# Constant products between the first transposes, and router products of two tiles ahead of the seventh projection

## The chip, the cores and the metric

The kernel runs on one core of one Trainium2 chip. A core has five engines that run side by side, each with its own instruction queue: TensorE (PE: matrix products and transposes), VectorE (DVE), ScalarE (ACT), GpSimd (POOL, here used to issue DMAs, among them the indirect ones) and SyncE (SP, which only issues DMAs). They signal each other with semaphores. The metric is the device time of one execution in microseconds; lower is better.

## The reference, cut to what matters

The program is one layer of a streaming encoder on 512 tokens of width 1024, with 16 learned meta tokens in front, all in float32:

```python
h   = rmsnorm(concat(meta, x), mix_norm)
u   = h @ w_in                      # 1024 -> 2304, split among three groups of heads
mix = concat(conv(u), windowed_attention(u), gated_recurrence(u))
r   = concat(meta, x) + mix @ w_out
n   = rmsnorm(r, ffn_norm)
group  = top1(softmax(n @ w_router_group + b));   expert = top2(softmax(n @ w_router_expert + b) in that group)
y   = sum of weight * (silu(n @ w_gate[e]) * (n @ w_up[e])) @ w_down[e] over the two experts
out = rmsnorm(r + y, final_norm)[16:]
```

There are 32 experts of 3 MB of weights each, and every one of them is loaded.

## The kernel before

**Mixer.** The 512 tokens are four tiles of 128 rows. In the beginning each tile of x is normalised (ScalarE: squares, Ln, Exp; DVE: the scaling, `normed_x`, L723) and transposed by TensorE in eight 128x128 blocks (`turn_tile`, L1220 to L1224); small parameters (L1234) and the meta tokens (L1238) are transposed too. DVE and ScalarE copy the transposes out, and `half_product` (L1226) starts the input projection with the gate columns: eight products over the 1024 inputs, each shown in the trace as two passes of 264 columns. The other projections, the convolution, the recurrence and the attention follow; TensorE's order is written out by hand in `mixer_tensor`.

**Output projection and router.** `project(i)` (L1442) is the output projection of tile i//2, half i%2 of the columns: eight products of 512 columns into bank 7, 16 passes in the trace (L1455). `residual(i)` (L923 to L930, DVE) adds bank 7 to the residual tile, and the next `project` waits for it, since all use bank 7. `second_norm(j)` (L653, ScalarE) makes the factor of the second norm. `normed_rows(j)` (L932 to L938, DVE) multiplies the tile by it and by the gain into `xf`; POOL then writes this tile to the memory tensor `normed` (L1551 to L1553). `router_turn(j, n)` transposes the two halves of the residual tile, `router_half` copies them out, and `router_of(j)` (L1496) does the router's products: eight products of only 36 columns, 16 passes in the trace (L1471). The seventh and eighth projection are `project(6)` and `project(7)`, the two halves of the last tile.

**Experts known early.** `select` (L957, DVE) turns the router's outputs of tiles 0 to 2 into picks. TensorE counts them (`early_ranks`, L1501), DVE and TensorE build lists from them (`early_rows`, `early_lists`, `early_index`), and POOL gathers rows of `normed` by these lists with an indirect DMA (`rows_in`, L2000 to L2006). POOL waits for the three written tiles (L2019) and for the index (L2020) before the first gather. The last tile takes the same path a little later: TensorE transposes the first gathered block (L1536, seen in the trace as L1560) ahead of the last four router products (L1538).

**Experts.** Weights go through a ring of seven slots. SP issues the load of a slot once TensorE's last block on it is done (L1638 to L1641). The first six experts' weights are asked for during the mixer, each behind the wait that frees its place: `load_down(5)` and `load_gate(5)` behind projection 6 (L468 to L470), `load_down(0)` and `load_up(5)` behind projection 7 (L471 to L473).

Banks are PSUM, TensorE's output memory. The queues are in order: on each engine an instruction that waits holds back all behind it.

Of the kernel before, what the change touches and what calls it, by code (L numbers as in the profile page):

```python
# [13 lines left out]
P = 128  # L14
D = 1024
KT = D // P
# [147 lines left out]
def trunk(nc, x, meta_tokens, mix_norm, w_in, conv_dw_w, conv_dw_b, conv_ln_g, conv_ln_b, attn_sinks,  # L164
# [3 lines left out]
    with ctx:  # L168

        def sb(name, shape, dt=F32, of=ctx):  # L170
            return of.enter_context(nc.sbuf_tensor(name, shape, dt))
# [4 lines left out]
        bank = [ctx.enter_context(nc.psum_tensor(f"bank{i}", [P, 512], F32)) for i in range(8)]  # L176
# [4 lines left out]
        cst = sb("cst", [P, K_ALL])  # L181
# [75 lines left out]
        ident = cst[:, K_ID:K_ID + P]  # L257
# [148 lines left out]
        def turned(j, k):  # L406

            c = k % 2 * 2 * P + j % 2 * P
            return bank[(2, 3, 4, 5)[k // 2] if j < 2 else (6, 7, 4, 5)[k // 2]][:, c:c + P]
# [293 lines left out]
        def mixer_vector(dve):  # L703
            vn = [0]

            def step(ins):
                vn[0] += 1
                ins.then_inc(v_step, 1)
                dve.wait_ge(v_step, vn[0])

            def mark(ins):
                vn[0] += 1
                ins.then_inc(v_step, 1)
                return vn[0]
# [31 lines left out]
            for i in range(2):  # L746
                n = f"a{i}"
# [175 lines left out]
            def residual(i):  # L923

                j, n = i // 2, i % 2
                dve.wait_ge(oproj, i + 1)
                if i == 0:
                    dve.wait_ge(d_resid, 16)
                h = xs[:, j, n * 512:(n + 1) * 512]
                V.tensor_tensor(h, h, bank[7][:, :], ALU.add).then_inc(h2_done, 1)  # L930

            def normed_rows(j):  # L932
                if j == 0:
                    dve.wait_ge(d_gain, 16)
                dve.wait_ge(h2_done, 2 * j + 2)
                dve.wait_ge(fstat, j + 1)
                V.scalar_tensor_tensor(out=xf[:, j, :], in0=xs[:, j, :], scalar=rstd[:, j:j + 1], in1=gain,
                                       op0=ALU.mult, op1=ALU.mult).then_inc(xf_ready, 1)  # L938

            def router_half(j, n=0):  # L940
                dve.wait_ge(xfT, 2 * j + n + 1)
                src = bank[TURN_BANK[j, n]][:, :].rearrange("p (k t) -> p k t", k=4)
                dst = mixT[:, 4 * n:4 * n + 4, j * P:(j + 1) * P] if j < NT - 1 or n else h_low
                V.tensor_copy(dst, src).then_inc(hfT_v, 1)
# [75 lines left out]
            def early_rows():  # L1020

                dve.wait_ge(ranks, 1)
                step(V.tensor_tensor(early_of, picked[:, :, 0:ET, 0:SLOTS],
                                     rank_early[:, :, 0:SLOTS].unsqueeze(1).to_broadcast([P, 2, ET, SLOTS]), ALU.mult))
                step(V.tensor_reduce(early_row, early_of, AX, ALU.add))
                by_row = [P, 2 * ET, ROWS_A]
                V.tensor_tensor(early_slot, cst[:, K_IOTA:K_IOTA + ROWS_A].unsqueeze(1).to_broadcast(by_row),
                                early_row.rearrange("p k j -> p (k j)").unsqueeze(2).to_broadcast(by_row), ALU.is_equal).then_inc(match, 1)
# [44 lines left out]
            router_half(2)  # L1073
            for k in range(2):
                mark(V.tensor_scalar(tok2[:, k], cst[:, K_TOK:K_TOK + NT], float(k * SEQ - FAR), None, ALU.add))
            normed_rows(2)
            select(range(ET), bank[0], ET)
            dve.wait_ge(picks, ET)
            dve.wait_ge(v_step, vn[0])
# [4 lines left out]
            mark(V.memset(sum3_late[:, 0:SLOTS], 0.0))  # L1084
            mark(V.tensor_copy(sum3_late[:, SLOTS:], sum3[:, SLOTS:]))
            residual(6)
            early_rows()
            router_half(3)
            early_index()
# [126 lines left out]
        def mixer_tensor(pe):  # L1216
            T = nc.tensor
            pe.wait_ge(d_cst, 16)

            def turn_tile(j):  # L1220
                pe.wait_ge(xn_ready, NORMS.index(j) + 1)
                for k in range(KT):
                    ins = T.transpose(turned(j, k), xs[:, j, k * P:(k + 1) * P], ident)
                ins.then_inc(xT_done, 1)  # L1224

            def half_product(n, h):  # L1226
# [2 lines left out]
                                   start=(k == 0), stop=(k == KT - 1))  # L1229
                return ins  # L1230

            turn_tile(0)
            pe.wait_ge(d_par, 112)
            T.transpose(bank[6][:, 0:86], rows[:, :], ident[0:86, 0:86]).then_inc(par_T, 1)  # L1234
            turn_tile(1)
            pe.wait_ge(xn_ready, NORMS.index(NT) + 1)
            for k in range(KT):
                ins = T.transpose(bank[7][:, k * META:(k + 1) * META], meta_x[:, k * P:(k + 1) * P], ident[0:META, 0:META])  # L1238
            ins.then_inc(metaT, 1)
            pe.wait_ge(d_win[0], 16)  # L1240
            pe.wait_ge(hT_v, 5)
            pe.wait_ge(hT_a, 4)
# [199 lines left out]
            def project(i, ks=range(KT)):  # L1442

                j, n = i // 2, i % 2
                if i == 0:
                    pe.wait_ge(y_c, 2)
                    pe.wait_ge(y_h, 2)
                if n == 0:
                    pe.wait_ge(y_a, 2 * j + 2)
                if j == 0:  # L1450
                    pe.wait_ge(d_wout[n], 16)
                if i >= 1:
                    pe.wait_ge(h2_done, i)
                for k in ks:
                    ins = T.matmul(bank[7][:, :], mixT[:, k, j * P:(j + 1) * P], w_out_sb[:, n, k, :],  # L1455
                                   start=(k == 0), stop=(k == KT - 1))
                if k == KT - 1:
                    ins.then_inc(oproj, 1)

            def router_turn(j, n):  # L1460
                pe.wait_ge(h2_done, 2 * j + n + 1)
                for k in range(4):
                    ins = T.transpose(bank[TURN_BANK[j, n]][:, k * P:(k + 1) * P], xs[:, j, (4 * n + k) * P:(4 * n + k + 1) * P], ident)
                ins.then_inc(xfT, 1)
# [31 lines left out]
            def router_of(j):  # L1496
                pe.wait_ge(hfT_a, j + 1)
                pe.wait_ge(hfT_v, j + 1)
                router(j, bank[0], range(KT)).then_inc(logits, 1)

            def early_ranks():  # L1501

                pe.wait_ge(picks, ET)
                o = bank[1]
                T.matmul(o[:, 0:3 * NE], tri, both[:, 0:3, :], start=True, stop=False)
                T.matmul(o[:, NE:3 * NE], ones, both[:, 0:2, :], start=False, stop=False)
                T.matmul(o[:, 2 * NE:3 * NE], ones, both[:, 0, :], start=False, stop=True).then_inc(ranks, 1)
# [12 lines left out]
            router_of(0)  # L1520
            router_turn(2, 0)
            router_turn(2, 1)
            project(6, range(KT // 2))
            router_of(1)
            router_of(2)
            project(6, range(KT // 2, KT))
            early_ranks()
            router_turn(3, 0)
            project(7, range(3))
# [543 lines left out]
        @block.vector  # L2073
        def _(dve):
            experts_vector(dve, *mixer_vector(dve))

        @block.tensor
        def _(pe):
            mixer_tensor(pe)
            experts_tensor(pe)  # L2080
# [33 lines left out]
```

## Time and profile before

| | us |
|---|---|
| median of 3 runs (lowest, highest) | 558.34 (555.75, 558.54) |
| profiled execution, its own time | 555.7 |
| span of its trace | 553.8 |
| TensorE busy | 489.0 (88%) |
| DVE busy | 247.0 (45%) |
| ScalarE busy | 152.3 (28%) |
| mean granted TensorE clock | 0.957 |
| bytes moved by DMA | 142.69 MB, mean 258 GB/s |

The span runs from the first to the last instruction; the profiled execution's own time is 1.9 us longer. Shares of busy time are averages over stages that have different limits. The page cuts the span into 40 slices of 13.8 us each and gives a digit for each. The groups of rows further down are read from the page and from the trace.

### The profile page before, as it was taken

The page shows a single profiled execution, that of the slowest core. Times are in us where ns is not written, and L with a number is a line of the kernel's source. Part 1 is how long each engine was busy: PE and PEld are TensorE (multiplying, and loading weights), DVE is VectorE, ACT ScalarE, POOL GpSimd, SP SyncE. Part 2 cuts the span into 40 slices and gives each one's busy share as a digit, 9 for nine tenths or more (in the row PEclk, how much of TensorE's full clock was granted, in tenths as well). Part 3 has the DMA queues.
Part 4 walks back from the last instruction along what each step waited for, and adds up shares of the span by engine and source line. Part 5 has one row for each costly group of instructions (what it writes and reads, how often), then busy time and mean ns, then how long its engine had stood idle before and what let it go on. Part 6 is the DMA issues. An engine that isn't in the chain of part 4 may idle for free. (4 is left out here: it accounts for less than half of the span.)

```text
span 553.8 us, 11004 instructions
## 1 busy us (share of the span) xinstructions
PE 489.0 (88%) x4555; PEld 310.6 (56%) x4555; DVE 247.0 (45%) x608; ACT 152.3 (28%) x375; POOL 40.0 (7%) x47
## 2 busy tenths in 40 slices
PE   3999999999999999999999999999999697856800
PEld 3885478875557656557476655655555354443400
DVE  3206995767236854634573333323332123112237
ACT  5410004766012623422033322222221112011123
POOL 0010000000001000000110111211112011000000
PEclk9999999999999999998999999999999899789865
DMA  7990000000007797008888999999999999999465
GB/s 264 363 351 1 2 0 2 0 1 1 2 1 228 278 423 299 39 38 290 347 302 327 340 418 392 402 415 413 419 413 415 410 413 416 410 415 408 176 261 209
DMA packets 38754, 142.69 MB, mean 258 GB/s; under 512 B 5170, under 2 KB 12584, under 8 KB 30384
## 3 DMA queue, kind: packets, MB, share of 16 engines
q1 hardware_dynamic: 31824, 127.89, 59.0%
q0 software_dynamic: 5760, 11.55, 5.8%
q10 hardware_dynamic: 1120, 2.54, 1.2%
q8 instruction: 37, 0.61, 0.4%
q14 instruction: 13, 0.11, 0.1%
HBM read 135.83 MB, written 15.20 MB: 273 GB/s over the span
## 5 line engine op out<-in xcount | busy, mean ns | idle before, releaser
L1455 PE MATMUL bank<-area_w,area_m 128*128 128x512 f32 x128 | 58.5, 609 | 0.4 <-issue 0.4
L1567 PE MATMUL bank<-area_g,area_m 128*64 128x256 f32 x352 | 47.0, 413 | 7.9 <-DMA area_g<-in_w_exp_up 7.9
L1567 PE MATMUL bank<-area_w,area_m 128*64 128x256 f32 x256 | 34.0, 408 | 7.4 <-DMA area_w<-in_w_exp_up 7.1
L1567 PEld LDWEIGHTS bank<-area_g,area_m 128*64 128x64 f32 x352 | 25.7, 147 | 25.3 <-issue 14.2
L762 DVE SCALAR_TENSOR_TENSOR area_m<-area_g,cols,area_m 128x512 f32<-128x512 f32 x60 | 39.8, 745 | 0.0
L1455 PEld LDWEIGHTS bank<-area_w,area_m 128*128 128x128 f32 x128 | 24.1, 195 | 27.5 <-issue 27.5
L1770 DVE COPY cst<-bank 128x128 f32<-128x128 f32 (+1 forms) x39 | 10.2, 260 | 59.2 <-PE bank L1584 39.9
L1286 PE MATMUL bank<-area_h,area_w 128*128 128x264 f32 x160 | 35.9, 386 | 0.0
L1286 PEld LDWEIGHTS bank<-area_h,area_w 128*128 128x128 f32 x160 | 30.4, 190 | 5.6 <-issue 0.5
L1320 PE MATMUL bank<-area_h,area_w 128*128 128x512 f32 x64 | 30.8, 612 | 0.0
L1567 PEld LDWEIGHTS bank<-area_w,area_m 128*64 128x64 f32 x256 | 18.9, 145 | 18.7 <-issue 11.7
L1288 PE MATMUL bank<-area_h,area_w 128*128 128x512 f32 x64 | 27.6, 592 | 0.0
L1704 ACT ACTIVATE cst<-bank 128x128 f32<-128x128 f32 x22 | 6.2, 280 | 74.5 <-PE bank L1567 74.5
L1788 DVE COPY area_m<-bank 64x512 f32<-64x512 f32 x20 | 13.9, 694 | 24.3 <-PE bank L1590 22.5
L2011 POOL DMA_INDIRECT expert_out<-area_m,cst x14 | 13.8, 987 | 150.1 <-DVE area_m L1791 107.6
L1575 PE MATMUL bank<-area_w,area_m 128*32 128x128 f32 x640 | 21.6, 275 | 2.5 <-DMA area_w<-in_w_exp_up 2.5
L1777 DVE TENSOR_TENSOR cst<-cst,bank 128x128 f32<-128x128 f32 x22 | 6.4, 289 | 38.1 <-ACT cst L1704 38.1
L1575 PEld LDWEIGHTS bank<-area_w,area_m 128*32 128x32 f32 x640 | 16.5, 109 | 8.9 <-issue 7.0
L1674 ACT ACTIVATE area_m<-bank 128x512 f32<-128x512 f32 x17 | 10.2, 599 | 40.6 <-PE bank L1560 34.7
L1278 PE MATMUL bank<-area_w,area_h 128*128 128x128 f32 (+1 forms) x128 | 21.3, 327 | 0.0
L1590 PE MATMUL bank<-area_g,cst 128*64 128x512 f32 x88 | 21.1, 599 | 0.0
L1288 PEld LDWEIGHTS bank<-area_h,area_w 128*128 128x128 f32 x64 | 12.2, 190 | 14.9 <-issue 14.8
(356 smaller groups left out, 780.6 us busy)
## 6 DMA issues: line engine op xcount, KB each, us to landing
area_w<-in_w_exp_gate SPq DMA_DIRECT2D x14, 1024.0 KB, 14.6
area_w<-in_w_exp_up SPq DMA_DIRECT2D x14, 1024.0 KB, 21.3
area_g<-in_w_exp_gate SPq DMA_DIRECT2D x14, 1024.0 KB, 15.8
area_g<-in_w_exp_up SPq DMA_DIRECT2D x14, 1024.0 KB, 23.2
area_g<-in_w_exp_down SPq DMA_DIRECT2D x14, 1024.0 KB, 23.2
area_w<-in_w_exp_down SPq DMA_DIRECT2D x14, 1024.0 KB, 22.5
area_w<-in_w_in SPq DMA_DIRECT2D x7, 1024.0 KB, 12.6
area_w<-in_w_out SPq DMA_DIRECT2D x2, 2048.0 KB, 12.4
```

The costliest lines, as they stand in the source:

```text
L762: ins = V.scalar_tensor_tensor(out=mixT[:, i, :], in0=src, scalar=w, in1=mixT[:, i, :], op0=ALU.mult, op1=ALU.add)
L1278: ins = T.matmul(out_b[:, n0:n0 + w], hT[:, k, t0:t0 + P], w_in_sb[:, k, c0:c0 + w], start=(k == 0), stop=(k == KT - 1))
L1286: ins = T.matmul(half_of(n, h), w, hT[:, k, h * HALF:(h + 1) * HALF], start=(k == 0), stop=(k == KT - 1))
L1288: ins = T.matmul(out_b[:, :], w, hT[:, k, META:], start=(k == 0), stop=(k == KT - 1))
L1320: ins = T.matmul(bank[QUERY_BANK[i]][:, :], w_in_sb[:, k, C_Q + i * P:C_Q + (i + 1) * P], hT[:, k, META:], start=(k == 0), stop=(k == KT - 1))
L1455: ins = T.matmul(bank[7][:, :], mixT[:, k, j * P:(j + 1) * P], w_out_sb[:, n, k, :], start=(k == 0), stop=(k == KT - 1))
L1567: ins = T.matmul(out_b[h * BC:(h + 1) * BC, 0:2 * P], x[:, k, :], w_gate_up[slot][:, :, k, h * P:(h + 1) * P], start=(k == 0), stop=(k == ...
L1575: ins = T.matmul(out_b[q * 32:(q + 1) * 32, 0:P], x[:, k, :], w_gate_up[slot][:, q // 2, k, q % 2 * P:(q % 2 + 1) * P], start=(k == 0), st ...
L1590: ins = T.matmul(out_b[n * BC:(n + 1) * BC, :], aT[:, f * BC:(f + 1) * BC], w_down[slot][:, f, n * 512:(n + 1) * 512], start=(f == 0), sto ...
L1674: A_.activation(xT_half(i, 0), bank_half(0)[:, :, 0:rows_of(i)], ACT.Copy).then_inc(xT_lo, 1)
L1788: V.tensor_copy(y_part(yb[k.i % 2], k.row, 1), src[BC:P, :]).then_inc(y_hi, 1)
L2011: Q.indirect_dma_start(expert_out, index_of(i, idx_es, idx_s), yb[i % 2], None, bounds_check=2 * SEQ - 1, oob_is_err=False).then_inc(d_sc[ ...
```

## The change

Three edits. `fill(n)` issues n products of the identity with 256 columns of the constant table (identity and ones) into bank 1, which nothing reads before the first input projection overwrites it; four stand ahead of the first tile's transposes, one behind them, three ahead of the first projection. TensorE now does the router products of tiles 1 and 2 ahead of the whole of `project(6)`, where it did the first half of the projection before them and the second behind them. And DVE does `normed_rows(2)` behind `residual(6)`, no longer ahead of `select`.

```diff
@@ mixer_vector
-            normed_rows(2)
             select(range(ET), bank[0], ET)
             dve.wait_ge(picks, ET)
...
             residual(6)
+            normed_rows(2)
             early_rows()
@@ mixer_tensor
+            def fill(n):
+
+                for _ in range(n):
+                    T.matmul(bank[1][:, 0:2 * P], ident, cst[:, 0:2 * P], start=True, stop=True)
+
+            fill(4)
             turn_tile(0)
+            fill(1)
             pe.wait_ge(d_par, 112)
             T.transpose(bank[6][:, 0:86], rows[:, :], ident[0:86, 0:86]).then_inc(par_T, 1)
             turn_tile(1)
...
             ins.then_inc(metaT, 1)
+            fill(3)
             pe.wait_ge(d_win[0], 16)
...
             router_turn(2, 1)
-            project(6, range(KT // 2))
             router_of(1)
             router_of(2)
-            project(6, range(KT // 2, KT))
+            project(6)
             early_ranks()
```

## Rows read from the trace of the kernel before

**Rows 1.** The page, part 2: two lines of the 40 slices, in tenths.
```profile
PEclk9999999999999999998999999999999899789865
DMA  7990000000007797008888999999999999999465
```

**Rows 2.** Busy time by stage: stage, length, engines' busy time, clock, DMA share, GB/s.
```profile
306.00:308.00 2.00, 2.00 (x19) 1.12 (x19) 0.50 (x3) 1.50 (x4) 0.57 (x1) 1.00 0.57 80
...
350.00:500.00 150.00, 133.75 (x1594) 78.16 (x1585) 40.55 (x99) 29.70 (x72) 19.09 (x19) 0.94 1.02 413
```

**Rows 3.** Timeline, 4 to 32 us: start, duration, engine, line, operation, idle before.
```profile
4.11 1.28 ACT L498 ACT_TABLE_LOAD   x1 [4.11 <-DMA cst<-in_table]
...
8.04 1.94 PE L1223 MATMUL bank<-cst,area_x 128*128 128x128 f32 x8 [8.04 <-DVE area_x L723]
...
10.54 1.97 PE L1223 MATMUL bank<-cst,area_x 128*128 128x128 f32 x8 [0.41 <-DVE area_x L723]
...
12.43 1.03 PE L1238 MATMUL bank<-cst,area_g 16*128 16x16 f32 x8
...
14.54 5.04 PEld L1228 LDWEIGHTS bank<-area_h,area_w 128*128 128x128 f32 x16 [1.19 <-DMA area_w<-in_w_in]
14.58 5.43 PE L1228 MATMUL bank<-area_h,area_w 128*128 128x264 f32 x16 [1.11 <-DVE area_h L739]
...
21.59 10.85 PE L1228 MATMUL bank<-area_h,area_w 128*128 128x264 f32 x48
```

**Rows 4.** Timeline of TensorE, 250 to 280 us.
```profile
252.80 3.60 PE L1455 MATMUL bank<-area_w,area_m 128*128 128x512 f32 x8
256.24 3.66 PE L1471 MATMUL bank<-cst,area_m 128*128 128x36 f32 x32
259.73 5.38 PE L1455 MATMUL bank<-area_w,area_m 128*128 128x512 f32 x8
265.37 0.46 PE L1505 MATMUL bank<-cst 128*128 128x96 f32 x2 [0.27 <-DVE cst L1003]
...
267.26 0.66 PE L1463 MATMUL bank<-cst,area_x 128*128 128x128 f32 x4 [1.03 <-DVE area_x L930]
267.75 2.74 PE L1455 MATMUL bank<-area_w,area_m 128*128 128x512 f32 x6
...
277.34 1.15 PE L1560 MATMUL bank<-cst,area_h 128*128 128x128 f32 x8
```

**Rows 5.** Busy time by stage, with the granted clock, around the second half projection.
```profile
260.00:266.00 6.00, 5.73 (x14) 2.34 (x13) 5.90 (x49) 0.00 (x0) 0.00 (x0) 0.72 1.00 410
```

**Rows 6.** Timeline of DVE, 255 to 268 us.
```profile
255.30 1.29 DVE L937 SCALAR_TENSOR_TENSOR area_h<-area_x,stat,gain_out 128x1024 f32<-128x1024 f32 x1 [1.89 <-ACT stat L657]
...
259.94 0.58 DVE L962 SCALAR_TENSOR_TENSOR cst<-bank,stat,rbias 128x36 f32<-128x36 f32 x3 [3.35 <-PE bank L1471]
...
264.76 0.56 DVE L1003 SCALAR_TENSOR_TENSOR cst<-cst 128x32 f32<-128x32 f32 x3
...
266.52 0.68 DVE L930 TENSOR_TENSOR area_x<-area_x,bank 128x512 f32<-128x512 f32 x1
```

**Rows 7.** DMAs: issues by POOL, share of queue 0 (262 to 263 us), time to landing.
```profile
256.88 0.53 POOL L1553 DMA_DIRECT2D normed<-area_h  x1 [11.73 <-DVE area_h L937]
272.92 1.07 POOL L2005 DMA_INDIRECT area_h<-normed,cols  x1 [15.51 <-DVE cols L1033]
...
DMA to landing us min/median/max: 2.9/2.9/8.3
...
q0 software_dynamic: 37, 0.15, 36.8%
...
area_h<-normed,cols POOLq DMA_INDIRECT x1, 4.4
...
area_h<-normed,cols POOLq DMA_INDIRECT x1, 6.0
```
The line of minimum, median and maximum is that of the writes to `normed` at L1553; the last two lines are the gathers issued at 272.92 and 274.30.

## The prediction

> **What bounds the kernel now.** I read four views in turn. The slices of the page first [rows 1]: the reader is to see that the DMA engines idle in the middle of the mixer and are full for the last half, and that the granted TensorE clock dips once in slice 19, at about 260 us. Then busy time by stage [rows 2]: in 306 to 308 us the DMA share is 0.57, from 350 to 500 us it is 1.02 at 413 GB/s. The kernel therefore has two parts. From 308 us on the stream of expert weights sets the end, and nothing changes in it. Ahead of that, each load waits for TensorE to free a slot, so a microsecond won or lost by TensorE before about 306 us moves the start of the full stream, and with it the end, one for one. Then the timeline of TensorE: from 14.58 us it works with almost no gap up to 265 us, so the mixer is TensorE's too and a gain at its start is carried through. Last, the timeline and the DMAs between 250 and 280 us, where the rest of the change lies.
>
> **Part 1, the eight constant products.** TensorE waits for nothing but the first table part, which has landed by 4.11 us, and then stands until 8.04 us [rows 3]. A 264-column pass takes 10.85/48 = 0.226 us in the 48 from 21.59 us on; the 16 from 14.58 us take 5.43 us instead of 3.62 [rows 3]. They begin near 0.45 us each and end at 0.226, the ratio of the two clock levels, 1.2 and 2.4 GHz: TensorE starts at the lower and reaches the upper inside this group. A constant product is two passes of 256 columns.
> - fill(4): 8 passes at 0.44 = 3.5 us, 4.1 to 7.6, in front of DVE's first tile at 8.04. Cost 0.
> - fill(1): 0.44 us at the upper level, 0.9 at the lower, in a group that ends at about 9.8 and whose successor waits for DVE until 10.54 [rows 3]. Cost 0 to 0.3.
> - fill(3): 6 passes, 1.3 or 2.6 us, from about 13.2. The product behind it could start at 14.54, when the first weights land [rows 3]. Cost 0.1 at the upper level, 1.5 at the lower.
>
> If the clock is up by 8 us and stays up, the 16 passes take 3.62 us: 1.8 won, 0.1 paid, so **-1.7 us**. Bounds: +1.5 (the clock doesn't rise, fill(3) is pure delay) and -3.6 (an execution in which all 16 passes would have run low, 16 x 0.226). I take -1.7, the value of this profile.
>
> The Trainium skill (TensorE: Matmul & The Clock Gate, "What's actually happening") says the array's default is the lower clock and that sustained activity releases it; by it fill(4) alone should raise the clock before the first transposes. The trace shows only the rise inside the first dense group, not what a filler does.
>
> **Part 2, the order of router products and the seventh projection.** Before: half projection 252.80 to 256.24, 32 router passes to 259.7, half projection to 265.1, ranks at 265.37 after the picks [rows 4]. The first half needed 3.44 us (0.43 a pass), the second 5.38: the mean granted clock of 260 to 266 us is 0.72, which is 3.4 us at the lower level [rows 5], a loss of 1.9. After: router passes 252.8 to 256.5, then 16 passes of projection, 6.9 us, and the same 1.7 to 1.9 of low clock, since the weak stretch is now longer, not shorter. TensorE reaches the ranks at 265.0 to 265.2. So the projection gains nothing by itself (-1.8 if the low stretch should vanish, +1.5 if the router passes themselves run low too). DVE's select starts at 256.6 instead of 259.94 and its picks are made at 262.0 instead of 265.3 [rows 6]; TensorE's wait of 0.27 goes. The larger effect: the residual of the seventh projection no longer queues behind the select (266.52) but follows the projection at 265.2, so TensorE's next transposes start at 266.0 instead of 267.26 [rows 4]. From there the eighth projection, lists and index come 1.2 us earlier, and TensorE reaches the transposes of the first gathered block at 276.1 instead of 277.34. Taken alone: **-1.2 us**.
>
> **Part 3, normed_rows(2) moved past select and residual(6).** It took 1.29 us at 255.30, where DVE waited anyway [rows 6]. Now it runs 265.8 to 267.1. Behind it wait early_rows (match at 268.1, needed by TensorE at 269.1: hidden) and, on POOL's queue, the write of that tile to memory, and behind that the first gather, which waits for three written tiles as well as for its index. Before, the write was issued at 256.88 and took 8.3 us [rows 7], long landed when the index came. Now it is issued at 267.1 + 0.3 = 267.4. How long? 2.9 us where the queues were empty, 8.3 where they were full; in the full case its packets got about 37% of the engines [rows 7]. SP's queue is full here until about 273.5 (the loads of two expert pieces and the spill). I take 6.5 us: it lands at 273.9, 1.0 us after the gather was issued before (272.92). Reissue 0.6: 274.5. The gather itself took 4.4 us with idle queues, 6.0 for the second one, whose packets met the loads that the eighth projection releases [rows 7]. Those loads now come 1.2 us earlier, at 274.8, on top of this gather: I take 6.0. It lands at 280.5. In the profile TensorE began those transposes at 277.34, exactly as the gather (272.92 + 4.4) landed; there is no slack to hide this. Result for Parts 2 and 3 together: 280.5 - 277.34 = **+3.1 us**; bounds -1.2 (2.9 and 4.4: TensorE is late, not the gather) and +5.0 (8.3 and 6.0). The last tile's router half stands behind these transposes, so its select, the order of the experts and their loads all move with it.
>
> The Trainium skill (DMA: Bandwidth & Descriptors, "Anatomy of one DMA") gives 2.0 us plus bytes over 436 GB/s, an estimate of 3.2 us for 512 KB, near the 2.9 of the empty queues. By it the write would be in time; that is the first rival, worked out from the rows below.
>
> **Sum.** 555.7 (the profiled execution) - 1.7 + 3.1 = 557.1. The median of the three runs, 558.34, lies 2.6 above that execution, so I forecast 558.34 + 1.4 = **559.7 us**.
>
> **Rivals.**
> - *The gather is in time.* For it: 2.9 us landings exist, and 1.2 us of TensorE time is really freed. Against: both at once need empty queues, and 267 to 273 us is the fullest stretch of the mixer. Then -1.7 - 1.2 = -2.9: 555.4; if the low-clock stretch vanishes as well, 553.7. Chance 0.28.
> - *Slower: TensorE cools while it waits for the gather.* It would stand from 276.1 to 280.5, and the router work behind it is weak too. If the clock falls there, the next dense group (first expert, 3.67 us from 279.7 now) runs at half rate, +1.7 as in [rows 5]: 558.34 + 1.4 + 1.7 = 561.4. [...] Against: part of that work lies beside DVE's select. Chance 0.17. The Trainium skill (the same clock page, "HAM oscillation") describes such waits; no row here has one of that length after 14 us.
> - *The filler doesn't raise the clock.* Part 1 gives 0 to +1.5, with the late gather 561.4 to 562.9. For it: the transposes from 8.04 on did not raise it before 14.5. Chance 0.1.
> - Forecast, late gather without cooling: 0.45, own range 557.6 to 561.8 (gather +1.0 to +5.0, start -1.7).
>
> **How the numbers follow.** 0.5% is 2.8 us, about what a measurement of this kernel can tell from no change. Faster by that (below 555.6): 0.6 of the first rival, a little of the forecast and of executions that start colder, 0.26. Slower (above 561.1): most of the second and third rival and the upper end of the forecast, 0.32. Rest 0.42. Range 554.2 to 563.4: it takes in the first rival's main value and the third one's upper end, and leaves out the gain with both clock stretches gone and the sum of all losses.
>
> **What would show it.** First dense products at 0.226 us a pass and ending at about 18.2 instead of 20.0: Part 1. Router products of tiles 1 and 2 before projection 6, select starting 3.3 us sooner relative to the last router product of tile 0: Part 2. The write of the third tile issued after the seventh residual, a landing of 6 to 8 us, and TensorE idle ahead of the gathered block's transposes with the DMA as releaser: Part 3. If that idle time is under 0.5 us, my main step is wrong. If the end doesn't move with the first expert's start, the reading of the DMA stream is wrong.

## The result and the profile after

The changed kernel takes 565.15 us (median of four runs, 564.55 to 566.60) against 558.34: ratio 1.0143, 95% interval 1.0109 to 1.0176, so 6 to 10 us slower. (Ratios and intervals here and below are estimated from the single runs, so they differ a little from the quotient of two medians, 1.0122 here.) The forecast was 559.7, with a range up to 563.4: the time lies above it. The profiled execution took 564.55 us (span 562.6) against 555.7 (span 553.8), 8.8 us more.

The page's slices answer to [rows 1]:
```profile
PEclk9999999999999999999869999999999999778965
DMA  8990000000009794029926999999999999999565
```
A slice is 14.07 us. That of 253 to 267 us has no dip of the clock now; the two behind it, to 295 us, have one instead, to 0.8 and 0.6. In the second of these the DMA row has a hole (0.2 instead of 0.8): the full stream begins later.

Busy time by stage, columns as in [rows 2]:
```profile
260.00:266.00 6.00, 5.81 (x22) 3.10 (x21) 5.47 (x22) 0.00 (x0) 0.53 (x1) 1.00 1.00 389
...
280.00:283.00 3.00, 0.25 (x1) 0.25 (x2) 0.00 (x0) 0.00 (x0) 0.00 (x0) 0.50 0.80 317
283.00:286.00 3.00, 3.00 (x16) 3.00 (x15) 0.00 (x0) 1.08 (x2) 0.00 (x0) 0.50 0.00 0
...
350.00:500.00 150.00, 134.29 (x1620) 78.34 (x1619) 40.75 (x100) 29.55 (x73) 21.11 (x21) 0.95 1.02 413
```
Against [rows 5] the clock of 260 to 266 us is 1.00 instead of 0.72. From 280 us TensorE has 0.50, the level of 1.2 GHz, and from 283 us the DMA engines move nothing. Both last until 290 us. Once full, the stream is what it was: 413 GB/s.

TensorE's timeline at the start, answering to [rows 3]:
```profile
8.90 1.97 PE L1223 MATMUL bank<-cst,area_x 128*128 128x128 f32 x8 [1.50 <-DVE area_x L723]
...
11.66 1.06 PE L1223 MATMUL bank<-cst,area_x 128*128 128x128 f32 x8
...
14.89 3.72 PE L1228 MATMUL bank<-area_h,area_w 128*128 128x264 f32 x16
...
20.20 10.85 PE L1228 MATMUL bank<-area_h,area_w 128*128 128x264 f32 x48
```
The first 16 passes take 3.72 us instead of 5.43 and the 48 begin 1.39 us sooner. The first tile's transposes still take 1.97 us in this execution; only the second tile's take 1.06.

TensorE's timeline around the rest of the change, answering to [rows 4]:
```profile
252.00 3.66 PE L1479 MATMUL bank<-cst,area_m 128*128 128x36 f32 x32
255.49 7.11 PE L1463 MATMUL bank<-area_w,area_m 128*128 128x512 f32 x16
...
263.39 0.66 PE L1471 MATMUL bank<-cst,area_x 128*128 128x128 f32 x4 [0.19 <-DVE area_x L930]
...
272.98 0.66 PE L1471 MATMUL bank<-cst,area_x 128*128 128x128 f32 x4
282.75 1.97 PE L1567 MATMUL bank<-cst,area_h 128*128 128x128 f32 x8 [9.11 <-DMA area_h<-normed,cols]
284.52 1.76 PE L1479 MATMUL bank<-cst,area_m 128*128 128x36 f32 x8
286.20 6.31 PE L1574 MATMUL bank<-area_w,area_m 128*64 128x256 f32 x32
292.44 0.22 PE L1866 MATMUL bank<-cst 128*32 128x1 f32 x2
```
Two more rows of TensorE's timeline before:
```profile
276.85 0.66 PE L1463 MATMUL bank<-cst,area_x 128*128 128x128 f32 x4
...
283.31 0.22 PE L1859 MATMUL bank<-cst 128*32 128x1 f32 x2
```
Up to 272.98 TensorE is 3.87 us ahead of before, where the same four transposes began at 276.85. Then it waits 9.11 us for the gathered block and works at half speed behind it. The last row of each timeline is the counts that follow the first expert's 32 passes. They began at 283.31 before and begin at 292.44 now: from 3.9 ahead to 9.1 behind, inside 20 us.

Who made it wait, in the timelines of POOL and of SP's queue, answering to [rows 7]:
```profile
264.82 0.53 POOL L1560 DMA_DIRECT2D normed<-area_h  x1 [20.48 <-DVE area_h L937]
274.46 1.07 POOL L2012 DMA_INDIRECT area_h<-normed,cols  x1 [9.10 <-DMA normed<-area_h]
...
DMA to landing us min/median/max: 2.9/2.9/8.8
```
```profile
262.64 0.38 SPq L429 DMA_DIRECT2D area_w<-in_w_exp_down  x1
263.06 1.10 SPq L419 DMA_DIRECT2D area_w<-in_w_exp_gate  x1
272.16 0.37 SPq L429 DMA_DIRECT2D area_w<-in_w_exp_down  x1
272.57 0.54 SPq L422 DMA_DIRECT2D area_w<-in_w_exp_up  x1
```
The line with three landings is that of the three writes to `normed`. The third tile's write is issued 1.8 us behind a pair of expert loads and lands 8.8 us later, the maximum. Only then does the gather go out, at 274.46, 1.9 us behind the next pair, and it takes 8.3 us (274.46 to 282.75).

### The profile page after: what moved, and what is told of

Its sections match the earlier page's. It is cut to its first block and busy times, and to the rows that moved or that the text cites. A ratio compares the mean times of both kernels' runs of the same rounds, so it can differ in the third digit from the quotient of the medians.

```text
span 562.6 us, 11034 instructions
## 1 busy us (share of the span) xinstructions
PE 493.6 (88%) x4571; PEld 315.3 (56%) x4571; DVE 246.4 (44%) x608; ACT 151.6 (27%) x375; POOL 40.0 (7%) x47
## 5 line engine op out<-in xcount | busy, mean ns | idle before, releaser
L1463 PE MATMUL bank<-area_w,area_m 128*128 128x512 f32 x128 | 56.7, 594 | 0.4 <-issue 0.4
L1574 PE MATMUL bank<-area_g,area_m 128*64 128x256 f32 x352 | 44.8, 398 | 6.4 <-DMA area_g<-in_w_exp_up 6.4
L1574 PE MATMUL bank<-area_w,area_m 128*64 128x256 f32 x256 | 35.6, 423 | 5.5 <-DMA area_w<-in_w_exp_up 5.5
L1294 PEld LDWEIGHTS bank<-area_h,area_w 128*128 128x128 f32 x160 | 30.4, 190 | 5.6 <-issue 0.5
L1567 PE MATMUL bank<-cst,area_h 128*128 128x128 f32 x128 | 20.3, 309 | 9.1 <-DMA area_h<-normed,cols 9.1
L1567 PEld LDWEIGHTS bank<-cst,area_h 128*128 128x128 f32 x128 | 17.5, 199 | 9.9 <-DMA area_h<-normed,cols 9.3
```

Source lines behind the costliest of these rows:

```text
L1294: ins = T.matmul(half_of(n, h), w, hT[:, k, h * HALF:(h + 1) * HALF], start=(k == 0), stop=(k == KT - 1))
L1567: ins = T.transpose(bank[2 + k // 4][:, (k % 4) * P:(k % 4 + 1) * P], cols_of[:, k, :], ident)
L1574: ins = T.matmul(out_b[h * BC:(h + 1) * BC, 0:2 * P], x[:, k, :], w_gate_up[slot][:, :, k, h * P:(h + 1) * P], start=(k == 0), stop=(k == ...
```

## Experiments

Ratios are to the kernel before, timed beside each; 95% intervals in brackets. Line numbers shift by a few between kernels; tiles and operations identify the rows.

**The moved write alone.**
```
             for k in range(2): mark(V.tensor_scalar(tok2 ...
-            normed_rows(2)
             select(range(ET), bank[0], ET)
...
             residual(6)
+            normed_rows(2)
```


> The kernel before with one edit: normed_rows(2) behind residual(6). Theory T (the moved tile write makes the first gather late, and TensorE then waits and cools): write issued at about 268.8, landing 8 to 9 us later, gather 6 to 8 us after that, so TensorE's transposes of the gathered block start near 284 to 286 instead of 277.3, with the wait ascribed to the gather, and the low clock behind it: 567 to 571 us, 9 to 12 above the kernel before. Rival R (the router order costs the time, the moved write is hidden): no wait ahead of the gathered block, 558 us.

568.05 us, ratio 1.0187 [1.0111, 1.0263], from 558.16 to 571.47 over five runs. The single move loses about as much as the whole change, but the fastest of the five runs, the profiled one, loses nothing. The spread is wide, so the same kernel was profiled once more:

> The kernel of e1 once more, for a second profile: e1's profiled execution took 558.2 us, its others 565.5 to 571.5. Theory: whether the first gather is issued ahead of or behind the loads that projection 8 releases decides. If this one is slow (565 or more), its gather stands behind those loads and takes 7 us or more, and TensorE waits 4 us or more; if fast, the gather takes 4 to 5.

It took 573.04 us (one run). Rows of POOL, TensorE and SP's queue in the two, the first at 558.16 us:
```profile
268.69 0.53 POOL L1553 DMA_DIRECT2D normed<-area_h  x1 [23.55 <-DVE area_h L937]
275.89 1.07 POOL L2005 DMA_INDIRECT area_h<-normed,cols  x1 [6.68 <-DMA normed<-area_h]
...
267.74 4.44 PE L1455 MATMUL bank<-area_w,area_m 128*128 128x512 f32 x6
...
277.72 0.37 SPq L429 DMA_DIRECT2D area_w<-in_w_exp_down  x1
...
280.14 1.16 PE L1560 MATMUL bank<-cst,area_h 128*128 128x128 f32 x8 [0.95 <-DMA area_h<-normed,cols]
```
and the second:
```profile
273.54 0.53 POOL L1553 DMA_DIRECT2D normed<-area_h  x1 [23.55 <-DVE area_h L937]
280.75 1.07 POOL L2005 DMA_INDIRECT area_h<-normed,cols  x1 [6.68 <-DMA normed<-area_h]
...
272.60 2.74 PE L1455 MATMUL bank<-area_w,area_m 128*128 128x512 f32 x6
...
280.88 0.37 SPq L429 DMA_DIRECT2D area_w<-in_w_exp_down  x1
...
290.64 1.97 PE L1560 MATMUL bank<-cst,area_h 128*128 128x128 f32 x8 [8.28 <-DMA area_h<-normed,cols]
```
In both the gather goes out 7.2 us behind the write, which lands in 6.4 us, not in the expected 8 to 9. Behind it the two part: the gather takes 4.25 us where it has 1.8 us of lead over the next loads, and 9.9 us where it has 0.13. The lead comes from TensorE's clock. These loads follow the eighth projection, and the first six passes of that took 4.44 us in the first profile and 2.74 in the second: 1.7 us lost to the lower level (the granted clock of 262 to 272 us was 0.83) kept the loads out of the gather's way. The gather was expected behind the loads in a slow execution; it stood just ahead of them and was slow all the same. The race is not the whole difference, though. The second profile is 4.85 us late at the write already (273.54 for 268.69), by lower clocks ahead of it (the first dense group took 6.73 us instead of 5.49, and the granted clock of 150 to 200 us was 0.93 instead of 1.00). The gather adds 5.6, the half-speed work behind the long wait 2.7, and the low clock in the last expert (below) 1.6. How the other runs divide was not seen.

**The order alone.**
```
-            project(6, range(KT // 2))
             router_of(1)
             router_of(2)
-            project(6, range(KT // 2, KT))
+            project(6)
```


> The kernel before with one edit: router products of tiles 1 and 2 ahead of the whole of projection 6; normed_rows(2) stays ahead of the select, no constant products. Theory T: write of the third tile issued at about 256.9 and landed by 266; first gather issued at about 269 instead of 272.9 with SP's queue still full, so it takes 6 to 8 us instead of 4.4 and lands at 276 to 277: 0 to 1.5 us faster, 557.5 us. Rival R: the order itself brings the loss, 565 us or more.

558.26 us, 0.9976 [0.9933, 1.002]: no change. Its TensorE timeline:
```profile
264.24 0.66 PE L1463 MATMUL bank<-cst,area_x 128*128 128x128 f32 x4 [0.19 <-DVE area_x L930]
...
275.98 1.16 PE L1559 MATMUL bank<-cst,area_h 128*128 128x128 f32 x8 [1.49 <-DMA area_h<-normed,cols]
...
278.36 4.92 PE L1566 MATMUL bank<-area_w,area_m 128*64 128x256 f32 x32
```
The order wins 3.0 us up to the transposes at 264.24 (267.26 before) and loses them again: the gather goes out 3.0 sooner (269.92) but takes 6.1 us instead of 4.4, so TensorE waits, and the clock is down when the first expert comes (4.92 us instead of 3.67). The counts come at 283.21, 0.1 before those of before.

**The constant products alone, and the first four alone.**
```
+            fill(4)
             turn_tile(0)
+            fill(1)
...
+            fill(3)
             pe.wait_ge(d_win[0], 16)
```


> The kernel before with one edit: the eight constant products. Theory T: first dense products at 0.226 us a pass from the start, the timeline behind them 0.8 to 1.4 us earlier, and the end with it: 557.2 us. Rival R2 (the early gain is lost again before the experts): dense products at 0.226 but no change of the end, 558.3 us.

556.08 us, 0.9956 [0.992, 0.9992]. First dense group 3.83 us, counts at 281.94: 1.37 sooner. This kernel has the old order of router products, and its TensorE timeline answers to [rows 4] a second time:
```profile
258.43 3.68 PE L1463 MATMUL bank<-area_w,area_m 128*128 128x512 f32 x8
264.08 0.46 PE L1513 MATMUL bank<-cst 128*128 128x96 f32 x2 [1.97 <-DVE cst L1003]
```
The half projection runs at the full clock here, and TensorE then waits 1.97 us for DVE's picks. The low stretch of [rows 5] only took the place of that wait and cost nothing.

With `fill(4)` only:

> e3 with only the first four constant products. Theory: they raise the clock by 8 us, but between 8 and 14.3 us TensorE is half idle, and without the last three products it falls again before the first projection: dense passes start near 0.45 us, the group takes 5.4 instead of 3.8 us, end as the kernel before. Rival: the first four are enough, 3.8 us and the same end as e3.

556.80 us, 0.9984 [0.9951, 1.0017]. Its timeline:
```profile
7.90 1.09 PE L1223 MATMUL bank<-cst,area_x 128*128 128x128 f32 x8 [0.81 <-DVE area_x L723]
...
14.28 5.51 PE L1228 MATMUL bank<-area_h,area_w 128*128 128x264 f32 x16 [1.24 <-DMA area_w<-in_w_in]
```
Four products raise the clock (eight transposes in 1.09 us, 1.94 before) but don't keep it: the first dense group is as slow as before. In this group the gain comes from the two small fills; the medians of the two kernels don't tell them apart.

**Only the moved write undone.** The changed kernel, `normed_rows(2)` back ahead of `select`.

> The change with normed_rows(2) put back ahead of the select. Theory T: no wait of 9 us ahead of the gathered block, no low clock from 283 to 291; the two gains add up: 555.5 to 557 us, some 9 below the changed kernel. Rival R: still above 563 us.

555.55 us, 0.9941 [0.9904, 0.9978]: the whole loss, and more, was Part 3. Two rows of its timelines:
```profile
268.59 1.07 POOL L2012 DMA_INDIRECT area_h<-normed,cols  x1 [12.46 <-DVE cols L1033]
...
277.09 5.29 PE L1574 MATMUL bank<-area_w,area_m 128*64 128x256 f32 x32 [0.40 <-issue]
```
As in the order alone, the gather takes 6.1 us (TensorE goes on at 274.71) and the first expert runs partly at the lower level (5.29 us instead of 3.67).

**The loads held until the gather has landed.** First those that the eighth projection releases:
```
             sp.wait_ge(oproj, 2 * NT)
+            sp.wait_ge(d_xg[0], 16)
             load_down(sp, of(0), 0, d_dn[0])
```


> The changed kernel, with SP's loads behind projection 8 (down of expert 0, up of expert 5, last spill) held until the first gather has landed. Theory T (the gather takes 8.3 us because those 2.5 MB are ahead of it in the DMA engines): gather 4.4 us again, TensorE's transposes of the gathered block at about 278.5 instead of 282.75, the end 4 us earlier than the changed kernel, more if the clock falls later. Rival G (a gather issued at that point is slow whatever runs beside it): 8 us as before, and the end later, since the held loads come late.

560.73 us, 1.0047 [1.0012, 1.0082]. Then those of the seventh and eighth:
```
             sp.wait_ge(oproj, 2 * NT - 1)
+            sp.wait_ge(d_xg[0], 16)
             load_down(sp, of(5), 5, d_dn[5])
```


> The changed kernel, with SP's loads behind projection 7 and projection 8 all held until the first gather has landed. Theory T (the write of the third tile takes 9 us because SP's queue is full): the write takes 4 to 6 us, the gather 4.4, TensorE starts on the gathered block at about 275, and the end is 7 to 9 us earlier than the changed kernel's, about the kernel before. Rival: the write stays at 9 us and only the gather is faster, so no more than e5 gives.

553.59 us, 0.9919 [0.9884, 0.9955]. Timelines, the eighth held:
```profile
264.51 0.53 POOL L1561 DMA_DIRECT2D normed<-area_h  x1 [20.48 <-DVE area_h L938]
274.30 1.07 POOL L2013 DMA_INDIRECT area_h<-normed,cols  x1 [9.25 <-DMA normed<-area_h]
...
278.78 1.97 PE L1568 MATMUL bank<-cst,area_h 128*128 128x128 f32 x8 [5.45 <-DMA area_h<-normed,cols]
```
and both held:
```profile
265.60 0.53 POOL L1561 DMA_DIRECT2D normed<-area_h  x1 [22.17 <-DVE area_h L938]
269.84 1.07 POOL L2013 DMA_INDIRECT area_h<-normed,cols  x1 [3.70 <-DVE cols L1034]
...
DMA to landing us min/median/max: 2.9/2.9/2.9
...
276.78 3.67 PE L1575 MATMUL bank<-area_w,area_m 128*64 128x256 f32 x32 [0.41 <-issue]
```
Holding the eighth's loads brings the gather from 8.3 to 4.5 us and leaves the write at 8.9. Holding both brings the write to 2.9 as well (the maximum of its three landings), the gather waits for its index only, and TensorE has no wait and no low clock there. Both prices of Part 3 were the expert loads issued just ahead. With those out of the way the moved write costs nothing: with the write in its old place and the same loads held the time is 553.79 us (below).

**TensorE kept busy through the wait.** The changed kernel with 18 and with 24 constant products of 256 columns into a free bank ahead of the wait for the gather:
```
             router_turn(3, 1)
+            for _ in range(18):
+                T.matmul(bank[4][:, 0:2 * P], ident, cst[:, 0:2 * P], start=True, stop=True)
             pe.wait_ge(d_xg[0], 16)
```


> The changed kernel, with 18 constant products (7.9 us at the upper clock) ahead of TensorE's wait for the first gather. The gather and its landing stay as they are. Theory T (the wait also costs the clock): no low clock from 282 to 291, the first expert's 32 passes 3.7 us instead of 6.3, the end 3.5 us earlier than the changed kernel. Rival (the low clock lies beside DVE's select and costs nothing): no change of the end.

> As e7, with 24 constant products (10.5 us) instead of 18: in e7 they ended 2.6 us ahead of the gather's landing, and the first expert still ran at the lower clock. Theory T: with the wait filled to its end, the first expert's 32 passes take 3.7 us instead of 6.3 and the end comes about 2.5 us earlier than e7's. Rival: the low clock costs nothing, end as e7.

563.01 us, 1.0088 [1.0052, 1.0124], and 563.78 us, 1.0111 [1.0061, 1.016]. The intervals overlap that of the changed kernel, so a gain over it is not shown in the times. The 18 fell short, in part because the gather took 9.5 us here (272.98 to 282.45) and not 8.3, for a reason left open: 2.57 us of waiting were left, the clock dropped, and the first expert took 6.30 us. The 24 reached to 282.9 and it took 3.67; transposes, router passes and first expert together took 5.87 us (5.97 before, 9.69 in the changed kernel). The counts come 2.50 us sooner than with 18 (288.76, 291.26), and yet the time is not better. The two ends, SP's last expert load and TensorE's last rows, with 18:
```profile
506.83 1.76 SPq L429 DMA_DIRECT2D area_g<-in_w_exp_down  x1
...
528.45 1.08 PE L1584 MATMUL bank<-area_g,area_m 128*32 128x128 f32 x32
529.46 1.94 PE L1599 MATMUL bank<-area_g,cst 128*64 128x512 f32 x8
```
with 24:
```profile
504.59 1.76 SPq L429 DMA_DIRECT2D area_g<-in_w_exp_down  x1
...
526.19 1.93 PE L1584 MATMUL bank<-area_g,area_m 128*32 128x128 f32 x32
528.05 2.72 PE L1599 MATMUL bank<-area_g,cst 128*64 128x512 f32 x8
```
The win of the clock arrives at the last load (2.24 of 2.50 us). There TensorE waits for weights between short bursts; with 24 its clock is low in the very last expert, and 1.6 us are given back. Over all 14 profiles the end lies 54.6 to 54.9 us behind the last load in the 9 whose last expert runs at the upper level, and 56.1 to 56.3 in the 5 where it doesn't. What decides it was not settled, nor whether it accounts for the medians of these two.

**Four such products with the write in its old place, and both loads held there.** On the kernel with only the moved write undone: 4 products ahead of the gather's wait, or the wait of SP as above.

> e4 (constant products at the start, new router order, normed_rows(2) in its old place) with four more constant products, 1.7 us, ahead of the wait for the first gather, where e4's TensorE stood 1.55 us and ran the next group at the lower clock (first expert 5.3 us instead of 3.7). Theory: the clock stays up, 1.5 us faster than e4, 4.5 to 6 us faster than the kernel before. Rival (the clock falls because of the router products, the fillers only delay): no faster than e4.

> e4 (constant products, new router order, normed_rows(2) in its old place) with SP's loads behind projections 7 and 8 held until the first gather has landed. Theory T: the gather is issued at 268.6 into queues that run empty, lands by 273.2, TensorE doesn't wait: transposes of the gathered block 1.5 to 2 us earlier than e8's 275.3, end at 551.5 to 552.5. Rival: the held loads are then late for the experts, no faster than e8.

553.74 us, 0.9944 [0.9907, 0.9982], and 553.79 us, 0.9922 [0.9888, 0.9956]. In the first, the products fill the wait and the first expert takes 3.67 us (counts 281.27, 1.0 sooner than without them); the expected 1.5 us over the kernel without them don't show in the ratios (0.9944 and 0.9941). In the second the counts come at 278.61, 4.7 us before those of the kernel before, and the expected 551.5 to 552.5 us was missed. Its last load (495.55) is only 3.5 us sooner than before (499.05): held loads are bytes moved later, and the DMA share of 265 to 275 us was 0.47. Its last expert ran at the low clock besides. These two, the changed kernel with both pairs of loads held and the one with only the move undone all beat the kernel before by their intervals (none reaches 1), and with it the changed one; among them the intervals tell nothing apart.

## Why the prediction was wrong

*What bounds the kernel* held. The last expert load moves with the counts of the first expert one for one: 9.0 for 9.1 us in the changed kernel, 7.8 for 8.0 with 18 products, 3.4 for 3.9 with the eighth's loads held. Only where both pairs were held is it less: 1.8 for 2.9, and 3.5 for 4.7.

*Part 1, -1.7.* Measured -1.4: 1.71 won in the group, 0.3 paid (the group begins at 14.89, not 14.58), since the first tile came 0.9 us late in this execution; in the profile of the constant products alone it began at 14.30. The Trainium skill (TensorE: Matmul & The Clock Gate, "What's actually happening") says sustained work releases the clock. The traces agree, but not always as early as the prediction took from it: with the constant products alone the first tile's transposes took 1.09 us, while in the changed kernel's profile they took 1.97 and only the second tile's took 1.06. The rival that the filler does nothing is refuted.

*Part 2, -1.2.* Too small; by the order alone it is -3.0 at the next transposes. The step that failed: "the same 1.7 to 1.9 of low clock". All 16 passes took 7.11 us at the full clock. That the order does this is not shown: with the old order the low stretch stood in the seventh projection in one profile (before), in the eighth in two (the moved write alone the first time, `fill(4)` only) and in neither in two; with the new order it was absent in eight profiles and stood in the seventh projection in one (both pairs held, 8.70 us for the 16 passes). I had also taken the low stretch of before for a loss, and it stood where TensorE would have waited 1.97 us for the picks. Sooner here only meant sooner at the gather: at the counts the order alone is worth 0.1 us, and its time is unchanged. The forecast had -1.2 left over there, since it gave the gather no cost for going out sooner.

*Part 3: the step that decided.* The mechanism was the one forecast, and both sizes were wrong: "I take 6.5 us" for the write and "I take 6.0" for the gather. Measured 8.8 and 8.3, both beyond what I had put as the bad end (8.3 and 6.0). The first was a middle of two rows when the row for a full queue, 8.3, was the nearer one. The second came from [rows 7]'s second gather, issued at 274.30, 1.7 us ahead of the loads (276.03 on SP's queue). With the loads moved sooner and the gather later, my own times left it a lead of only 0.3 (274.5 and 274.8), and I kept the price of the row with 1.7. It went out 1.9 us behind them instead. The Trainium skill (DMA: Bandwidth & Descriptors, "Anatomy of one DMA") gives an estimate of 3.2 us for the write alone; the traces show something near it (2.9) for the first two writes of every profile, and for this third one only with both pairs of loads held. Behind the loads the 8.8 of the trace decides.

*The cooling rival (0.17) came true on top of the forecast.* I had priced it at 1.7 for one dense group. The transposes, the router passes and the first expert together took 9.69 us instead of 5.97: +3.7.

The sum, at the first expert's counts: forecast +1.4; Part 2 and the start, -0.9 (the write issued at 264.82, not 265.7); the write and its reissue 9.64 for 7.1, +2.5; the gather 8.3 for 6.0, +2.3; the cold clock, +3.7; in all +9.0, measured +9.1, and +8.8 at the end. The forecast and the cooling rival were no alternatives: the one was the cause of the other, and the cost of the clock should have stood in the sum beside the wait.

Of the marks set for the steps, these came: dense passes at 0.23 us, router products ahead of projection 6, TensorE idle with the DMA as releaser, and an end that moves with the first expert. The landing of "6 to 8 us" did not; it was 8.8.

## What to carry to other kernels

A small write that gates a later transfer is worth where it stands in the queues, not what it costs its engine: 1.3 us of DVE work moved behind a residual cost 1.7 to 1.9% of the kernel, because the write then stood behind loads of weights, and its gather behind or just ahead of the next ones. When a step is moved, write down the issue times of everything on all DMA queues around it, and take the slow row if it comes out behind a load. A TensorE wait ahead of dense work can cost more than its length: 9.11 us of waiting brought 3.7 us of half-speed work behind it, and the waits of 1.49 and 1.55 us in two of these kernels 1.3 and 1.6 in the first expert.

## What was not expected

- The same 128-row write lands in 2.9 us with the loads held, 6.4 when issued 4.8 us behind a pair of loads, and 8.8 to 8.9 when issued 1.8 us behind it. The distance isn't all: in its old place it stands 4.9 us behind the last of four loads and 4.2 behind a spill, and takes 8.5 (only the moved write undone).
- A gather takes 4.25 us or 9.9 in one and the same program, with 1.8 or 0.13 us of lead over the next loads. There, too, more than the lead counts: with 3.1 us of lead it took 4.4 us before and 6.1 with the new order, where it goes out 6 us behind the previous pair instead of 7.4.
- In 5 of 14 profiles the clock is low in the last expert, which costs about 1.5 us at the very end.
- The kernel before runs from 553.7 to 563.0 us (87 runs); the changed kernel with both pairs of loads held from 551.8 to 554.4 (10 runs), and the one with the write in its old place and both held from 551.9 to 556.6 (12 runs). What widens the former was not taken apart.
